# The last boundary between output projection and feed-forward, in two halves of 128 tokens

## What is computed

```python
y_x, y_c = token_mixer(u_x, u_c, w_in[l], ..., not last)      # its last step: acc @ w_out
h_x = h_x + mod_x[:, :, 5] * rms_norm(y_x, g[3])
h_x = _ffn_sublayer(h_x, mod_x, 2, g[4], g[5], ffn_w_gate[l, 1], ffn_w_up[l, 1], ffn_w_down[l, 1])

def _ffn_sublayer(h, mod, k, g_pre, g_post, wg, wu, wd):
    u = rms_norm(h, g_pre) * (1.0 + mod[:, :, 3 * k + 1]) + mod[:, :, 3 * k]
    return h + 0.5 * mod[:, :, 3 * k + 2] * rms_norm(swiglu(u, wg, wu, wd), g_post)
```

## Time and profile before

| | us |
|---|---|
| median of 3 runs | 2470.17 |
| lowest, highest | 2467.44, 2471.24 |
| the profiled execution | 2472.7 |
| its span | 2470.9 |
| granted TensorE clock, mean | 0.996 |

### The profile page before, as it was taken

How to read it: one execution, slowest core, us unless ns; L and a number is a source line. 1 busy time by engine, 2 the same in 40 slices (tenths; PEclk the granted TensorE clock), 3 DMA queues, 4 the chain that set the end, 5 groups by cost and what they waited for, 6 DMA issues and landing times.

```text
span 2470.9 us, 32886 instructions
## 1 busy us (share of the span) xinstructions
PE 2422.0 (98%) x12940; PEld 1989.9 (81%) x12940; DVE 1612.9 (65%) x2732; ACT 1076.4 (44%) x1894; POOL 29.5 (1%) x43
## 2 busy tenths in 40 slices
PE   9999999999999999999999999999999999999998
PEld 7888889877767676788888898888898788778887
DVE  5889887354455456678988884333465466578875
ACT  5222335455455535462223352222355565556444
POOL 0000000000000000000000000000001000000000
PEclk9999999999999999999999999999999999999999
DMA  6665553222322122226565523222234243233554
GB/s 266 238 215 206 194 197 121 100 69 69 103 69 77 60 69 86 77 78 221 201 216 196 191 85 116 94 100 88 95 115 157 78 150 124 86 120 135 188 178 156
DMA packets 97641, 332.53 MB, mean 135 GB/s; under 512 B 10960, under 2 KB 12112, under 8 KB 95824
## 3 DMA queue, kind: packets, MB, share of 16 engines
q1 hardware_dynamic: 97488, 330.43, 38.9%
HBM read 324.10 MB, written 6.29 MB: 134 GB/s over the span
## 4 chain that ended last, share of the span: by engine, by line
PE 90%; DVE 4%; ACT 3%; issue 1%; DMA 1%; SPq 0%; DVEq 0%; ACTq 0%
PE ps L359 26%; PE ps L350 22%; PE ps L351 21%; PE ps L384 4%; PE ps L836 4%; PE ps L1740 3%; PE ps L1715 3%; PE ps L1725 3%; PE ps L905 1%; ACT w_high L333 1%; DVE w_low L339 1%; DMA mod_first<-in_mods_first 1%; PE ps L370 1%; PE ps L369 1%; PE ps L376 0%
## 5 line engine op out<-in xcount | busy, mean ns | idle before, releaser
L339 DVE TENSOR_TENSOR w_low<-raw,w_high 128x1024 fp32r<-128x1024 f32 (+1 forms) x488 | 551.6, 1137 | 441.5 <-ACT w_high L333 440.5
L333 ACT ACTIVATE w_high<-raw 128x1024 fp32r<-128x1024 f32 (+1 forms) x488 | 481.0, 989 | 684.2 <-DMA raw<-in_weights 684.0
L350 PE MATMUL ps<-u_high,w_high 128*128 128x512 f32 (+1 forms) x1904 | 694.0, 372 | 3.0 <-DVE acc L2003 1.7
L351 PE MATMUL ps<-u_low,w_high 128*128 128x512 f32 (+1 forms) x1904 | 686.1, 368 | 0.0
L359 PE MATMUL ps<-u_high,w_low 128*128 128x512 f32 (+1 forms) x2496 | 541.6, 361 | 1.1 <-DVE w_low L339 1.0
L359 PEld LDWEIGHTS ps<-u_high,w_low 128*128 128x128 f32 x2496 | 424.0, 189 | 90.6 <-issue 18.9
L350 PEld LDWEIGHTS ps<-u_high,w_high 128*128 128x128 f32 x1904 | 358.6, 188 | 87.3 <-issue 16.5
L351 PEld LDWEIGHTS ps<-u_low,w_high 128*128 128x128 f32 x1904 | 358.9, 188 | 58.2
L452 DVE CUSTOM_DVE_ANT_0 ps<-mod_raw,c_all,smalls 128x1024 f32<-128x1024 f32 x256 | 319.2, 1287 | 1.6 <-DMA mod_raw<-in_mods 1.0
L350 PE MATMUL ps<-hid_high,w_high 128*128 128x512 f32 x462 | 179.7, 389 | 0.0
L351 PE MATMUL ps<-hid_low,w_high 128*128 128x512 f32 x462 | 179.7, 389 | 0.0
(11 more groups left out here) (236 smaller groups left out, 2782.6 us busy)
## 6 DMA issues: line engine op xcount, KB each, us to landing
raw<-in_weights SPq DMA_DIRECT2D x360, 512.0 KB, 3.5
mod_raw<-in_mods SPq DMA_DIRECT2D x128, 512.0 KB, 4.0
raw<-in_weights SPq DMA_DIRECT2D x64, 384.0 KB, 3.0
raw<-in_weights SPq DMA_DIRECT2D x64, 320.0 KB, 3.0
mod_first<-in_mods_first SPq DMA_DIRECT2D x8, 1024.0 KB, 20.0
h_kept<-h SPq DMA_DIRECT2D x16, 256.0 KB, 2.0
na_bias<-in_na_rows SPq DMA_DIRECT2D x16, 256.0 KB, 3.9
h<-h_kept SPq DMA_DIRECT2D x2, 2048.0 KB, 8.7
```

The source lines that it names most:

```text
L333: act.activation(w_high[s][:, 0:width], raw[s][:, 0:width], ACT.Copy).then_inc(high_made.sem, 1)
L339: dve.tensor_tensor(w_low[s][:, 0:width], raw[s][:, 0:width], w_high[s][:, 0:width], ALU.subtract).then_inc(low_made.sem, 1)
L350: pe.matmul(o, w_high[s][:, w], x_high(x), start=first and a == 0, stop=False)
L351: pe.matmul(o, w_high[s][:, w], x_low(x), start=False, stop=False)
```

## The change

`self.tail` is now [6, 7] for every Out, the last layer's too, so its last two rows are made in halves of 128 tokens and HalfNorm takes the place of Norm there. Where HalfNorm spoke of the halves x and c, it now speaks of `self.result.half(i)`: 256 columns where T is 512, 128 columns where it is 256. The filler products go. The head keeps high and low side by side; a matmul now takes 2 x 128 columns, of the high and of the low part, so there are 96 of them instead of 48. The six head units get places of their own (three more), and may be fetched from the first Out row on. Their splits into low parts stand behind the last tile of the second half.

```diff
-HEAD_SLOTS = ((4, 5), (6, 5), (4, 5), (6, 5), (6, 5), (4, 5))
+HEAD_SLOTS = ((4, 5), (6, 5), (4, 5), (6, 5), (6, 5), (4, 5, 6, 7, 8, 9))
...
-        stage = [i for i, n0 in enumerate(starts) if n0 <= n < n0 + EXTRA]
+        stage = [i for i, n0 in enumerate(starts) if n0 <= n < n0 + len(HEAD_SLOTS[i])]
...
-            free.append(n0 - 4 if n == n0 or stage[0] % 3 == 2 else n0 - 3)
+            free.append(n0 - 7 if stage[0] == 5 else n0 - 4 if n == n0 or stage[0] == 2 else n0 - 3)
...
+        for i in range(3):
+            raw.append(place(f"raw{7 + i}", [8, P], F32, big + 64 * KB + 8 * KB * i))
+            w_low.append(place(f"w_low{7 + i}", [8, P], F32R, big + 64 * KB + 8 * KB * i))
+            w_high.append(place(f"w_high{7 + i}", [8, P], F32R, big + 68 * KB + 8 * KB * i))
...
-                self.beside = False
+                self.beside = T == S_X
...
-                    dve.tensor_tensor(u_low[:, k, half(i)], sq[:, k % 2, half(i)], u_high[:, k, half(i)], ALU.subtract).then_inc(self.low[i].sem, 1)
+                    into = both_parts(u_high[:, k])[:, 1, self.result.half(i)] if self.beside else u_low[:, k, self.result.half(i)]
+                    dve.tensor_tensor(into, sq[:, k % 2, self.result.half(i)], u_high[:, k, self.result.half(i)], ALU.subtract).then_inc(self.low[i].sem, 1)
...
+            def head_beside(self, pe, banks):
+
+                def turn(e, k, i):
+                    cols = self.result.half(i)
+                    pe.matmul(both_parts(ps[:, banks[e]])[:, :, cols], w_high[SLOT_OF[self.n0 + e]][:, k], both_parts(u_high[:, k])[:, :, cols],
+                              start=k == 0 and i == 0, stop=False)
+
+                joins = HALF_JOINS["Out"]
+                for k in range(KT):
+                    pe.wait_ge(self.low[0].sem, self.low[0].at(k + 1))
+                    for e in range(HEAD):
+                        if joins[e] == k:
+                            pe.wait_ge(high_made.sem, self.n0 + e + 1)
+                        for kk in range(k + 1) if joins[e] == k else [k] if joins[e] < k else []:
+                            turn(e, kk, 0)
+                    if k == 2:
+                        self.result.sum_squares_of_c(pe)
+                    if k == 3:
+                        self.result.sum_products_of_c(pe)
+                for k in range(KT):
+                    pe.wait_ge(self.low[1].sem, self.low[1].at(k + 1))
+                    for e in range(HEAD):
+                        turn(e, k, 1)
...
-                self.tail = [] if self.T == S_X else [KT - 1] if j != 1 else [KT - 2, KT - 1]
+                self.tail = [KT - 2, KT - 1] if j == 1 else [KT - 1] if self.T > S_X else []
...
+            def half(self, i):
+
+                return slice(self.T // 2 * i, self.T // 2 * (i + 1))
```

More of the change, by code:

```diff
@@ L302, in build @@
         c_back = signals.new("c_back", 16)
-        landed = [signals.new(f"weights_landed{i}", 0) for i in range(SLOTS + EXTRA + 1)]
+        landed = [signals.new(f"weights_landed{i}", 0) for i in range(len(raw))]
         high_made = signals.new("weights_high_made", 0)
@@ L754, in tile @@
                     act.wait_ge(self.low[i].sem, self.low[i].at(k - 1))
-                act.activation(sq[:, k % 2, cols], tmp[:, k % 2, cols], ACT.Identity, bias=mod[:, self.shift + k, i:i + 1],
-                               scale=pre[:, 3 * self.l + self.j, k, i:i + 1]).then_inc(self.whole[i].sem, 1)
+                act.activation(sq[:, k % 2, cols], tmp[:, k % 2, cols], ACT.Identity, bias=mod[:, self.shift + k, c:c + 1],
+                               scale=pre[:, 3 * self.l + self.j, k, c:c + 1]).then_inc(self.whole[i].sem, 1)
                 act.wait_ge(self.whole[i].sem, self.whole[i].at(k + 1))
@@ L813, in power_step @@
             def power_step(self, dve, i, step):
-                cols, steps, summed = half(i), self.steps[i], self.result.summed[i]
+                cols, steps, summed = self.result.half(i), self.steps[i], self.result.summed[i]
                 r = rstd[:, 0, cols]
@@ L819, in power_step @@
                     dve.wait_ge(summed.sem, summed.at(2 + i))
-                    of = ps[:, 4, half(0)] if i else ps[:, 2, half(0)]
+                    of = ps[:, 4, self.result.half(0)] if i else ps[:, 2, self.result.half(0)]
                     dve.tensor_tensor(ssq[:, cols], of, r, ALU.mult).then_inc(steps.sem, 1)
@@ L825, in power_step @@
                     dve.wait_ge(summed.sem, summed.at(3))
-                    of = ps[:, 4, half(1)] if i else ps[:, 3, half(0)]
+                    of = ps[:, 4, self.result.half(1)] if i else ps[:, 3, self.result.half(0)]
                     dve.scalar_tensor_tensor(out=ssq[:, cols], in0=of, scalar=2.0, in1=ssq[:, cols], op0=ALU.mult, op1=ALU.add).then_inc(steps.sem, 1)
@@ L835, in turn @@
                 def turn(e, k, x, i):
-                    pe.matmul(ps[:, banks[e], half(i)], w_high[SLOT_OF[self.n0 + e]][:, k], x[:, k, half(i)],
+                    pe.matmul(ps[:, banks[e], self.result.half(i)], w_high[SLOT_OF[self.n0 + e]][:, k], x[:, k, self.result.half(i)],
                               start=k == 0 and x is u_high and i == 0, stop=False)
+                if self.beside:
+                    self.head_beside(pe, banks)
+                    return
                 joins = HALF_JOINS["Out" if self.j == 2 else "Down"]
@@ L1218, in take_x @@
             def take_x(self, act, m):
-                b, cols = m % 2, half(0)
+                b, cols = m % 2, self.half(0)
                 z, gain = ps[:, b, cols], post[:, 3 * self.l + self.j, m, 0:1]
@@ L1229, in take_c @@
             def take_c(self, act, m, n):
-                b, cols = m % 2, half(1)
-                z, gain = ps[:, self.half_bank(m, 1), cols], post[:, 3 * self.l + self.j, m, 1:2]
+                b, c, cols = m % 2, 1 if self.T > S_X else 0, self.half(1)
+                z, gain = ps[:, self.half_bank(m, 1), cols], post[:, 3 * self.l + self.j, m, c:c + 1]
                 act.wait_ge(used.sem, n + 1)
@@ L1254, in add_c @@
             def add_c(self, dve, m):
-                b, t, cols = m % 2, m - self.tail[0], half(1)
+                b, t, cols = m % 2, m - self.tail[0], self.half(1)
                 if m < KT - 1:
@@ L1271, in sum_squares_of_x @@
             def sum_squares_of_x(self, pe):
-                out, cols = ps[:, 7, half(0)], half(0)
+                out, cols = ps[:, 7, self.half(0)], self.half(0)
                 pe.wait_ge(self.squares.sem, self.squares.at(KT - 1))
@@ L1279, in sum_products_of_x @@
             def sum_products_of_x(self, pe):
-                cols = half(0)
+                cols = self.half(0)
                 pe.wait_ge(self.energies.sem, self.energies.at(KT))
@@ L1287, in sum_squares_of_c @@
             def sum_squares_of_c(self, pe):
-                out, cols, t = ps[:, 5, half(0)], half(1), len(self.tail)
+                out, cols, t = ps[:, 5, self.half(0)], self.half(1), len(self.tail)
                 if t > 1:
@@ L1296, in sum_products_of_c @@
             def sum_products_of_c(self, pe):
-                cols, t = half(1), len(self.tail)
+                cols, t = self.half(1), len(self.tail)
                 pe.wait_ge(self.c_energies.sem, self.c_energies.at(t))
-                pe.matmul(ps[:, 4, half(0)], ones[:, :], energy[:, cols], start=True, stop=True).then_inc(self.summed[1].sem, 1)
+                pe.matmul(ps[:, 4, self.half(0)], ones[:, :], energy[:, cols], start=True, stop=True).then_inc(self.summed[1].sem, 1)
                 pe.wait_ge(self.c_crosses.sem, self.c_crosses.at(t))
-                pe.matmul(ps[:, 4, half(1)], ones[:, :], cross[:, cols], start=True, stop=True).then_inc(self.summed[1].sem, 1)
+                pe.matmul(ps[:, 4, self.half(1)], ones[:, :], cross[:, cols], start=True, stop=True).then_inc(self.summed[1].sem, 1)
         class Down(Result):
```

28 lines of the change are left out of this document (15 added, 13 removed).

## The result

The changed kernel takes 2480.83 us (median of 7 runs, 2477.41 to 2482.92), the kernel before, measured beside it, 2471.24 (7 runs). The ratio is 1.0036, with a 95% interval of 1.0026 to 1.0045: slower by 8.9 us (6.4 to 11.1). The forecast was 2478.5, which is +8.3.

The account below looks back on a forecast made before the run. TensorE, busy 98% of 2470.9 us, was taken as the bound, with VectorE's chain setting the boundary. VectorE +10.8, places -1.9 and clock -0.6 gave +8.3 on 2470.2: 2478.5 us, own range 2475.5 to 2481 (0.60), overall 2475 to 2487.

Parts of the forecast that it names:

- Short fp32r matmuls: Out rows 6 and 7 on TensorE: 96 matmuls of 128 columns at 0.112 us each, 10.8 us instead of 5.8.
- The rival at the fp32 rate: Out rows on TensorE: short matmuls run at the fp32 rate, 0.21 us each; +15.9, 2486; chance 0.22.
- The first tile: Start of HalfNorm's tiles: first u low at 2266.6 (now 2266.97), the half ready 0.6 us earlier, no more.
- Half tiles: VectorE's u tiles: 0.94 us per half tile, sixteen 15 us against 11.7 for eight whole; last low 2286.2, now 2277.49.
- Two rivals: VectorE's tiles: cheaper passes, 0.168 an issue, +4.8, 2475.0, chance 0.10; TensorE sets the pace, -5.8, 2464.4, chance 0.06.
- The splits: VectorE behind the last tile: all six w_low splits take 6.89 us; VectorE through at 2293.3, 10.8 us later.
- What comes back: At n0+8: places load units early, so it follows VectorE by 11.2 us instead of 13.05; 1.9 us back.
- The rival "the places do nothing": Head units' places: units land late, the 1.9 us stay lost, +10.2, 2480.4; inside the forecast's range, no separate chance.
- The clock: TensorE groups from 2295.50: 1.7 us lost to the slow clock before; 0.6 us of it taken as coming back.

Follow-up runs that it names:

- e4: The changed kernel with Out rows 6 and 7 whole again (48 matmuls of 256 columns), HalfNorm still in halves; ratio 1.0053 on the kernel before, +13.1 us.
- e3: The changed kernel with four of six w_low splits moved from behind the last tile into VectorE's idle times; ratio 1.0015 on the kernel before, +3.7 us.
- e2: The changed kernel without the added places: units 4 and 5 in places of their own, the rest in the ring; ratio 1.0046 on before, +11.4 us.
- e8: The changed kernel with ScalarE making w_high of n0+6 to n0+9 right behind the last tile, ahead of the silus; ratio 1.0037 on before, +9.1 us.
- e11: The changed kernel with the edits of e3, e5 and e8 together; ratio 1.0016 on the kernel before, +4.0 us.
- e5: The changed kernel with TensorE's sums of the second half moved from k = 2 and 3 of the head to 0 and 1; ratio 1.0040 on before, +9.9 us.
- e6: The changed kernel with 24 more 128-column VectorE passes into memory nobody reads; ratio 1.0056 on the kernel before, +13.8 us.
- e12: The kernel before, without places, with ScalarE making w_high of n0+6 to n0+9 ahead of the silus; ratio 1.0034 on before, +8.4 us.
- e1: The kernel before with only the six places of their own; Norm, whole rows and filler stay; ratio 0.9995 on before, -1.2 us.
- e7: The kernel before with the six places and ScalarE making w_high of n0+6 to n0+9 ahead of the silus; ratio 0.9996 on before, -1.0 us.
- e9: The changed kernel with six filler products on TensorE right ahead of n0+6; ratio 1.0043 on the kernel before, +10.6 us.
- e10: The kernel before with three filler products ahead of n0+6 and three ahead of n0+8; ratio 0.9997 on before, -0.7 us.

## Why the prediction was right

- **Direction and size** held: +8.9 by the ratio (median 2480.83) against +8.3, inside 2475 to 2487.
- **Short fp32r matmuls.** 16 of them from 2255.47 to 2257.21 are 0.109 each, the eight lows (2257.21 to 2258.10) 0.111; I took 0.112 from the earlier trace rows. The rival at the fp32 rate is out. The rate that the Trainium skill gives in "TensorE: Matmul & The Clock Gate", section "Back-to-back issue gap", about 81 ns at 128 columns, is not reached; the measurement decides.
- **The first tile** was forecast at 2266.6 - 2253.89 = 12.7 us of the stretch and came at 12.52. Its working had one step too many: ScalarE's wait for row 6 of the second half, behind 72 matmuls, does not bind (e4). What binds is the sum behind 56 of them and ScalarE's own queue after it. So the price of the fp32 rival, 72 x 0.1, rested on the wrong count as well.
- **Half tiles** were taken at 0.94 and took 0.93; the last u low was forecast at 32.3 and came at 31.98, with the root's wait of 2.60 us (3.60 in layer 0) and the clock's lower level where layer 0 had them. Two rivals fall by these rows: a pass is issued every 0.20 us, not 0.168, and 0.93 a half tile is above the 0.72 at which TensorE would have set the pace. The Trainium skill, "VectorE: DVE Perf Modes", section "The TRN2 errata — SBUF-src ops pay a fixed extra latency per instruction", gives (N + 151) / 0.96 ns for an fp32 tensor_tensor. An estimate from it is 291 ns for 128 and 424 for 256 columns; the rows' 0.29 and 0.42 agree.
- **The splits** took 6.89 us in one piece; VectorE was through 10.5 us later, forecast 10.8. e3 shows that 4.4 of this was only their place.
- **What comes back.** n0+8 follows VectorE by 50.23 - 39.00 = 11.23 us, forecast 11.2: 1.9 back, exactly, and for the wrong reason. I gave it to the places; e2 has no places and its n0+6 comes as early (43.65), since with VectorE 10 us late the ring's transfers are in time. The rival "the places do nothing" was right in that, and wrong in its price: the 1.9 come back all the same. That n0+6 waits for ScalarE behind two silus was not foreseen, and e8 shows that it cost nothing.
- **The clock** was the mis-sized term: 0.6 back, where n0+8 and n0+9 took 2302.72 - 2295.50 = 7.2 us before and 2311.39 - 2305.70 = 5.7 after: 1.5 back. The trace's sum is 10.5 - 1.9 = 8.6, less 1.5 and 0.2 further back: +6.9. The time gave +8.9, nearer to 8.6 with nothing back. The clocks of the timed runs fit that loosely: after averages 0.9956, where e3 and e11, with the halves but without the long wait, have 0.9964, so some of its runs seem to lose the clock that its one trace kept. I had read a term from one execution that single executions do not settle.
- **Luck.** That the total came within 0.6 us of the forecast is in part luck: the trace's own sum is 1.4 below it, the time is 2.0 above the trace. The long tail of before's one trace would explain those 2.0, but no row shows it.

**A faster version.** Neither kernel with the places beats before beyond its interval (0.9995 with 0.9986 to 1.0004, and 0.9996 with 0.9987 to 1.0005); both are clearly faster than the changed kernel. What the places alone gain is at most 3.5 us and may be nothing.

## What to carry to other kernels

Cutting a stage in halves pays only if the engine that feeds it has room: VectorE's passes cost 0.20 us at 128 columns and 0.335 at 256, so sixteen half tiles cost 15 us where eight whole ones cost 12, whatever TensorE saves in waiting. When a step is made from another stage's template, look at everything that the template queues behind it: more than half of this loss went when four splits left the place that another boundary's order had given them. And a wait's releaser names who came last, not who is late: take it away in thought, and ask what the next one is.

## What the hardware showed that was not expected

- TensorE's same instructions ahead of the boundary end between 2251.2 and 2256.7 us in fourteen traces; two traces can be compared to a fraction of a microsecond only from a common point close by.
- TensorE's clock behind a wait of 2.4 us or more ahead of n0+6: in six of seven traces (e2, e4, e5, e6, e8, e12) the first group takes 3.65 to 3.78 us, that is, it runs at the lower level; in the changed kernel's own it takes 2.08 behind 3.31 us of waiting. In the kernel before 2.66 us stand behind a wait of 1.91 (n0+8), but 2.06 behind one of 1.82 (n0+6). With waits of 1.06 us and less (e1, e3, e7, e11) or filler in the wait (e9, e10) the group takes 2.06 to 2.14.
